# A two-layer decoder trunk: every product of the dense layers split into high and low parts, with low parts on GpSimd and vector accumulators in PSUM banks

## The reference, cut to what matters

```python
for l in range(DEPTH):                     # DEPTH = 2
    mod = silu(c) @ ada_w[l] + ada_b[l]    # shift, scale and gate of both sub-layers
    hn = rmsnorm(x) * (1 + sc1) + sh1
    xr, yr, ga, gb, gate_a, gate_b = split(hn @ w_in[l], 6)          # 1024 x 6144
    xc = short_conv(xr, 4 taps)
    h = rg_lru(xc)                         # two block-diagonal gates, then a linear recurrence
    ya = (gelu(yr) * h) @ w_branch_a[l]
    v = long_conv(ga * sigmoid(gb), 31 taps)
    yb = silu(layernorm(v)) @ w_branch_b[l] + b_branch_b[l]
    x = x + (1 + g1) * ((sigmoid(gate_a) * ya + sigmoid(gate_b) * yb) @ w_out[l])
    hn2 = rmsnorm(x) * (1 + sc2) + sh2
    x = x + (1 + g2) * (swiglu(hn2) if l == 0 else moe_top2_of_8(hn2))
y = rmsnorm(x)
```

## Time and profile before

| | us |
|---|---|
| median of 3 runs | 1646.33 (1645.79 to 1647.4) |
| the profiled execution | 1645.37 |
| its span, first to last instruction | 1643.2 |
| TensorE busy in the span | 1510.4 (92%) |
| DVE busy | 1060.5 (65%) |
| ScalarE busy | 696.6 (42%) |
| GpSimd busy | 3.6 (0%) |

### The profile page before, as it was taken

The page is one execution under the profiler, slowest core; times in us unless marked ns, Lnnn a source line. Parts: engine busy times, 40 slices in busy tenths (PEclk is TensorE's granted clock), DMA queues, the critical chain, the costliest instruction groups (busy, mean ns, idle before and its releaser), DMA issues.

```text
span 1643.2 us, 22612 instructions
## 1 busy us (share of the span) xinstructions
PE 1510.4 (92%) x8980; PEld 1291.2 (79%) x8980; DVE 1060.5 (65%) x1546; ACT 696.6 (42%) x836; POOL 3.6 (0%) x12
## 2 busy tenths in 40 slices
PE   5899999689899999989999788759999999999996
PEld 3556677579798989956777578749999999999995
DVE  2247894466544443335796477457888887898886
ACT  3134311353433332223511044335666666666662
POOL 0000000000000000000000000000000000000000
PEclk9999999789999999999999989859999999999998
DMA  9754535945476754352343944308778878877880
GB/s 343 247 179 152 207 113 109 139 129 182 194 292 230 270 179 129 116 94 86 118 125 121 86 140 146 154 36 307 285 281 305 330 277 313 324 288 284 304 319 33
DMA packets 103765, 327.32 MB, mean 199 GB/s; under 512 B 58000, under 2 KB 59408, under 8 KB 86416
## 3 DMA queue, kind: packets, MB, share of 16 engines
q1 hardware_dynamic: 103696, 326.37, 60.1%
HBM read 322.52 MB, written 3.82 MB: 199 GB/s over the span
## 4 chain that ended last, share of the span: by engine, by line
PE 84%; DVE 5%; SPq 3%; ACT 3%; DMA 3%; issue 1%; DVEq 0%; ACTq 0%
PE ps L483 23%; PE ps L466 8%; PE ps L468 7%; PE ps L467 7%; PE ps L697 6%; PE ps L698 6%; PE ps L699 6%; PE ps L663 3%; PE ps L725 3%; PE ps L727 3%; PE ps L726 3%; PE ps L508 3%; SPq L383 2%; DMA raw<-in_stream 2%; PE ps L524 2%; PE ps L516 1%
## 5 line engine op out<-in xcount | busy, mean ns | idle before, releaser
L483 PE MATMUL ps<-hn,raw 128*128 128x320 f32 x1536 | 424.5, 438 | 9.1 <-ACT hn L802 6.0
L483 PEld LDWEIGHTS ps<-hn,raw 128*128 128x128 f32 x1536 | 293.8, 192 | 137.7 <-issue 16.9
L1032 DVE TENSOR_TENSOR mlo<-mraw,mhi 128x2816 fp32r<-128x2816 f32 x108 | 332.6, 3086 | 26.1 <-ACT mhi L962 24.3
L962 ACT ACTIVATE mhi<-mraw 128x2816 fp32r<-128x2816 f32 x108 | 275.7, 2555 | 31.4 <-PE ps L699 30.1
L1032 DVE TENSOR_TENSOR wlo<-raw,whi 128x1024 fp32r<-128x1024 f32 x114 | 139.0, 1223 | 208.8 <-ACT whi L760 208.7
L1097 DVE SCALAR_TENSOR_TENSOR v<-ub,cols,v 128x320 f32<-128x320 f32 x480 | 224.4, 545 | 0.0
L760 ACT ACTIVATE whi<-raw 128x1024 fp32r<-128x1024 f32 x114 | 120.3, 1055 | 174.5 <-PE ps L468 101.4
L697 PE MATMUL ps<-mhi,xg_hi 128*128 128x352 f32 x576 | 187.6, 326 | 2.6 <-DVE xg_lo L1032 2.6
L698 PE MATMUL ps<-mlo,xg_hi 128*128 128x352 f32 x576 | 185.4, 322 | 0.0
L699 PE MATMUL ps<-mhi,xg_lo 128*128 128x352 f32 x576 | 185.3, 322 | 0.0
L466 PE MATMUL ps<-xn_hi,whi 128*128 128x320 f32 x480 | 151.6, 316 | 7.0 <-DVE xn_lo L1032 6.8
(11 more groups left out here) (218 smaller groups left out, 2138.8 us busy)
## 6 DMA issues: line engine op xcount, KB each, us to landing
mraw<-in_moe SPq DMA_DIRECT2D x108, 1408.0 KB, 6.8
raw<-in_stream SPq DMA_DIRECT2D x210, 512.0 KB, 3.6
ada<-in_ada SPq DMA_DIRECT2D x24, 2048.0 KB, 8.2
out_cc<-upad SPq DMA_DIRECT2D x18, 120.0 KB, 13.0
wrg<-in_wrg SPq DMA_DIRECT2D x2, 1024.0 KB, 19.4
upad<-in_cc SPq DMA_DIRECT2D x16, 120.0 KB, 3.3
x<-in_x SPq DMA_DIRECT2D x1, 1280.0 KB, 7.8
out_y<-bb SPq DMA_DIRECT2D x8, 160.0 KB, 1.9
```

Of the source, the lines that this page charges most:

```text
L483: mm = e.matmul(ps[s][:, 0:T], raw[:, s, k * P:(k + 1) * P], hn[:, k, :], start=k == 0, stop=k == NT - 1)
L962: e.activation(mhi[:, s % MSPL, :], mraw[:, s % MRAW, :], ACT.Copy).then_inc(m_hi, 1)
L1032: return e.tensor_tensor(out, src, hi.bitcast(F32), ALU.subtract)
```

## The change

All chunks are now split; `native` and the buffer `hn` are gone. The layer's order becomes four chunks of gates and values for the long convolution, then the short convolution's inputs, then the other gates and values. ScalarE makes every high part. The low parts of the input projection and of branch a (chunks 0 to 55 of each layer) are made by GpSimd, those of branch b, the output projection and the SwiGLU by DVE. Loads wait for these low parts.

Chunks go round three PSUM banks instead of four. The banks set free hold vector data: the running sums of both convolutions (DVE's taps now read one operand from SBUF and one from PSUM; ScalarE writes the first tap of the long one), values and merged branches that are used straight from their bank, the roots and reciprocals of the norms. ScalarE also takes over the casts to high parts of activations and one square. The first two chunks of a stage are multiplied together, tile by tile (`ramp`). The RG-LRU gates stand one pair behind each of chunks 14 to 21. The sums over v stand behind chunks 28, 38, 46 and 53, and the squares of the layer norm are summed behind chunk 55, after branch a. The state stores are issued one behind each chunk load from chunk 36 on. The adaLN slices of layer 0 use one buffer, with one slice every three chunks.

```diff
-XR, GG, YR, GA, GB, BA, BB, WO = 0, 8, 24, 32, 40, 48, 56, 64
-IN_STREAM = {XR: 16, GG: 0, YR: 24, GA: 32, GB: 48, BA: 40, BB: 56, WO: 64}
-
-NATIVE = 48
+G0, XR, G1, YR, GA, GB, BA, BB, WO = 0, 4, 12, 24, 32, 40, 48, 56, 64
+IN_STREAM = {G0: 0, XR: 16, G1: 4, YR: 24, GA: 32, GB: 48, BA: 40, BB: 56, WO: 64}
...
+BANKS = 3
...
+LO_POOL = {n: k + 1 for k, n in enumerate(n for n in range(NCHUNK) if place_of(n)[1] < BB)}
+LO_DVE = {n: k + 1 for k, n in enumerate(n for n in range(NCHUNK) if place_of(n)[1] >= BB)}
...
+        SPREADS = ({2: (0,), 3: (1,), 15: (2, 3), 23: (4, 5), 36: (6, 7)},
+                   {2: (0,), 3: (1,), 18: (2, 3), 26: (4, 5), 38: (6, 7)})
...
+        def bank(n):
+            return ps[n % BANKS][:, 0:T]
...
+            def run_and_store(l, n0, n1):
+
+                for n in range(n0, n1):
+                    chunk(L0[l] + n)
+                    if 0 <= n - 36 < 2 + NT:
+                        store_state(l, n - 36)
+                store_state(l, 2 + NT)
...
+            def low(n):
+                e.wait_ge(hi_ready, n + 1)
+                e.tensor_tensor(wlo[:, n % RING, :], raw[:, n % RING, :], whi[:, n % RING, :].bitcast(F32),
+                                ALU.subtract).then_inc(lo_pool, 1)
...
+                for n in range(RING, BB):
+                    low(L0[l] + n)
...
+            def begin(n):
+                e.wait_ge(*split_done(n))
+                if n >= BANKS:
+                    e.wait_ge(*emptied(n - BANKS))
...
+            def ramp(n, xs, ready):
+
+                begin(n)
+                begin(n + 1)
+                for k in range(NT):
+                    e.wait_ge(*ready(k))
+                    for m in (n, n + 1):
+                        mm = split_mm(bank(m), wtile(m, k), (xs[0][:, k, :], xs[1][:, k, :]), k == 0, k == NT - 1)
+                        if k == NT - 1:
+                            mm.then_inc(chunk_done, 1)
...
+                ramp(p0, xn, lambda k: (norm_ready, HN_BASE[2 * l] + k + 1))
+                slice_of(1)
+                for n in range(2, BA):
+                    paired(p0 + n, xn)
+                    slice_of(n)
+                    if 14 <= n < 22:
+                        gates(n - 14)
+                    if n in (28, 38, 46):
+                        sum_v((28, 38, 46).index(n))
...
+                    paired(p0 + n, q, (lambda k: (q_ready, 2 * l + k // 4 + 1)) if n == BA else None)
+                    if n == BB - 3:
+                        sum_v(3)
+                sum_squares()
+                ramp(p0 + BB, q, lambda k: (v_ready, NT * l + k + 1))
+                for n in range(BB + 2, WO):
+                    paired(p0 + n, q)
...
+                def evac_gate(i):
+                    if i >= 2 or l:
+                        e.wait_ge(u_ready, NT * l + i - 1)
+                    if i < 2 and l:
+                        e.wait_ge(h_ready, NF)
+                    evacuate(p0 + gate_of(i), tmp[:, i % 2, :], ACT.Sigmoid)
...
+                    e.wait_ge(spread_done, NT * l + i + 1)
+                    e.activation(segs(ps[CONV[i % 2]][:, 0:T], TS), segs(out[:], CW)[:, :, 0:TS], ACT.Identity,
+                                 scale=col("ccw", l, i), bias=col("ccb", l, i)).then_inc(seeded, 1)
...
+                    ahead(p0 + n)
+                    slice_of(n)
+                    if 14 <= n < 22:
+                        i = n - 14
+                        for w, (buf, b) in enumerate(((ab, "ba"), (bb, "bx"))):
+                            e.wait_ge(rg_done, 2 * NT * l + 2 * i + w + 1)
+                            e.activation(buf[:, i, :], ps[SHORT[w]][:, 0:T], ACT.Sigmoid, bias=col(b, l, i)
+                                         ).then_inc(rg_sig, 1)
...
+                    for i in SPREADS[l].get(n, ()):
+                        spread(i)
...
+                    if n == BB - 2:
...
+            def tap(out, src, w, acc, since=1):
+
+                if conv_n[0] > since:
+                    e.wait_ge(conv_step, conv_n[0] - since)
+                return e.scalar_tensor_tensor(out=segs(out, TS), in0=src, scalar=w, in1=segs(acc, TS), op0=ALU.mult,
+                                              op1=ALU.add)
...
+                    n = p0 + gate_of(i)
+                    e.wait_ge(evac_done, EVAC[n])
+                    e.wait_ge(chunk_done, n + 2)
+                    g, val = tmp[:, i % 2, :], bank(n + 1)
...
+                    for k in range(1, KC):
+                        for do in between.get(k, ()):
+                            do()
+                        for j in range(2):
+                            t = i + j
+                            acc = ps[CONV[j]][:, 0:T]
+                            src = segs(ub[j][:], CW)[:, :, k:k + TS]
+                            w = col("ccw", l, k * NT + t)
+                            if k == 1:
+                                e.wait_ge(seeded, NT * l + t + 1)
+                            if k < KC - 1:
+                                step(tap(acc, src, w, acc))
+                            else:
+                                tap(v[:, t, :], src, w, acc, 1 - j).then_inc(v_done, 1)
...
+                    long_conv(0, {10: (sh(0),), 14: (sh(1),), 18: (sh(2),), 22: (sh(3),), 25: (u(2),)})
+                    make_u(3)
+                    long_conv(1, {10: (u(4),), 20: (u(5),), 30: (u(6),)})
+                    long_conv(2, {2: (u(7),), 6: (decay,)})
...
+                    long_conv(0, {8: (sh(0),), 11: (sh(1),), 13: (sh(2),), 16: (sh(3),), 18: (u(2),), 25: (u(3),)})
+                    make_u(4)
+                    long_conv(1, {8: (u(5),), 15: (u(6),), 21: (u(7),)})
+                    decay()
+                    long_conv(2, {})
+                recur()
...
-                long_conv(3, {20: lambda: wlow(p0 + BA), 24: lambda: wlow(p0 + BA + 1), 28: lambda: wlow(p0 + BA + 2)})
-                for n in range(BA + 3, BA + 6):
+                long_conv(3, {})
...
+                for i in range(NT):
+                    e.scalar_tensor_tensor(out=v[:, i, :], in0=ps[5][:, 0:T], scalar=-1.0 / D, in1=v[:, i, :],
+                                           op0=ALU.mult, op1=ALU.add).then_inc(ln_cent, 1)
+                for n in range(BB, BB + 4):
                     wlow(p0 + n)
...
-                        wlow(p0 + BB + (i + 1) // 2)
...
+                    n = p0 + BB + i
+                    e.wait_ge(chunk_done, n + 1)
+                    link(e.scalar_tensor_tensor(out=bank(n), in0=bank(n), scalar=col("bbb", l, i), in1=sgb[:, i, :],
+                                                op0=ALU.add, op1=ALU.mult))
+                    e.tensor_tensor(bank(n), bank(n), gy[:, i, :], ALU.add).then_inc(m_sum, 1)
+                    e.wait_ge(m_high, NT * l + i + 1)
+                    low(1, xn_lo[:, i, :], xn_hi[:, i, :], bank(n)).then_inc(m_ready, 1)
+                    wlow(n + 4)
```

More of the change, by code:

```diff
@@ L396, in _ @@
-            store_states(0)
-            run(BA, WO)
-            e.wait_ge(out_done, STORES)
+            e.dma_start(adas[0][0][:], ada[NA]).then_inc(ada_landed[0], 16)
+            run(RING, 9)
+            for g in range(NSLICE - NA - 1):
+                e.wait_ge(ada_rows, NA + g + 1)
+                e.dma_start(adas[0][0][:], ada[NA + g + 1]).then_inc(ada_landed[0], 16)
+                run(9 + 3 * g, 12 + 3 * g)
+            run_and_store(0, 9 + 3 * (NSLICE - NA - 1), BB)
+            run(BB, WO)
@@ L560, in sum_v @@
-                def sum_v(i):
-                    e.wait_ge(conv_step, CONVS * l + C_SHORT + 2 * KC * (i // 2 + 1))
-                    return e.matmul(ps[4][:, 0:T], ones[:], v[:, i, :], start=i == 0, stop=i == NT - 1)
-                for n in range(GA):
-                    native(p0 + n, NT * 2 * l if n == 0 else None)
-                    if l == 0:
-                        if n == 1:
-                            rows(NA - 1, NA, 32, adas[0][NA - 1])
-                        if n == 2:
-                            turn(NA)
-                        if n % 4 == 3 and NA + 1 + n // 4 < NSLICE:
-                            rows(NA, NA + 1 + n // 4, 16 * (n // 4 + 1), adas[0][NA])
-                        if n % 4 == 1 and n > 4 and NA + n // 4 < NSLICE:
-                            turn(NA + n // 4)
-                    if n == 11:
-                        gates()
@@ L596, in _, with slice_of, gates @@
-                for n in range(BB, WO):
-                    paired(p0 + n, (q_hi, q_lo), (lambda k: (v_ready, NT * l + k + 1)) if n == BB else None)
+                def slice_of(n):
+                    if l == 0 and n <= 22 and n % 3 == 1:
+                        rows(0, NA + n // 3, 16 * (2 + n // 3), adas[0][0])
+                    if l == 0 and n <= 23 and n % 3 == 2:
+                        turn(NA + n // 3)
+                def gates(i):
+                    if i == 0:
+                        e.wait_ge(wrg_in, 16 * (l + 1))
+                        e.wait_ge(xc_ready, NT * (l + 1))
```

(29 more changed lines are left out.)

625 lines of the change are left out of this document (291 added, 334 removed).

## The result

The changed kernel takes 1536.45 us (median; 1534.24 to 1538.87) against 1646.06 for the kernel before: the ratio is 0.9335 with a 95% interval of 0.9318 to 0.9351. The prediction was 1542 us, faster. The profiled execution has a span of 1537.1 us, 106.1 less than before.

What follows compares the result with a forecast made beforehand. TensorE, busy 92% of the span, was taken as the bound. Gains of 59.1 us in layer 0 and 57.5 in layer 1 make 116.6; 1645.4 - 116.6 + 13 charged = 1542 us, range 1518 to 1580.

Steps and rivals of the forecast that it cites:

- rival A: Whole kernel: TensorE's chunk rate sets the pace, 1542 us, with 1522 to 1556 of its own; chance 0.62.
- charges: Taken off the gain: stores 3 + 3 us, u tiles 2, ScalarE's lumps 5; together 13 us.
- Chunk price: TensorE: a split chunk takes 3.52 us against 4.31 for a native one, 0.79 us cheaper.
- Layer 0's stretch: Layer 0's input projection on TensorE: 195.1 us against 236.0, 40.9 us less.
- The pause: TensorE idle while state stores hold SP's queue: spreading them gains 15.2 and 15.4 us, less 3 us a layer charged.
- Branch a and the layer norm: Stretch behind the input projection: 29.3 us plus a 9.2 us chain, 38.5 against 41.5, 3.0 us less a layer.
- DVE's cover: Input projections: DVE's work, with PSUM taps at 0.48 us, is just in time; 2 and some 10 us to spare.
- rival C: DVE and GpSimd sharing SBUF: each of 12 DVE instructions waits out a whole low part; 1575 us; chance 0.09.
- GpSimd's cover: GpSimd's low part takes 2.68 us, 3.7 with the high part, against 10.6 us between buffer release and use.
- Rival D: GpSimd's low part sets the pace: no gain at about 5.0 us each, 1693 us at 5.5; chance 0.07.
- Rival E: State stores stall TensorE in their new place, 15 us a layer: 24 more, 1566 us; chance 0.09.
- B: Convolution taps in PSUM come at 0.549 us on DVE: 1556 us; chance 0.13.

Runs made afterwards that it cites:

- the third edit: Changed kernel with three TensorE waits taken away; this one delays layer 1's second low part until the samples are modulated. All three together: 1532.73 us, ratio 0.9312.
- the first run: Kernel before with only the state stores moved, one behind each weight chunk from chunk 36 on, native chunks kept: 1608.16 us, ratio 0.9762.
- run 44: Not a run number: 44 counts low parts. The run meant is the changed kernel with SBUF accumulators and low parts cut to 32 columns: 1586.76 us, ratio 0.9615.

## Why the prediction came out right

The code's way was as predicted (rival A), and the time within 0.4%. Without its charges the forecast had a span of 1643.2 - 116.6 = 1526.6; the charges were 13 us, and the measured span lies 10.5 above. The parts were less right than the sum, and that it fits so closely is in part luck: the 6 us charged for the stores were not needed, and other waits, which follow, took their place.

**Chunk price: right.** 4.31 to 3.52 us. No run changes it alone: 94 chunks at 0.79 less are 74 us, and the rest of the change behind the stores is 71.7. Layer 1's stretch took 184.4 us from its first matmul against 187.3 - 1.5 = 185.8.

**Layer 0's stretch: 202.7, not 195.1.** 4.16 of the 7.6 are the last u tile. The step charged 2 us for u tiles, thinking of a DVE that is late. DVE had idled: that u stood behind pair 2's first taps, which waited 17.37 and 1.58 us for ScalarE's spreads (DVE's timeline; upad is the u tile). ScalarE made these from 175.24 on, behind sixteen tanh and exp instructions that began at 165.54: it is the lump for which 5 us were charged, and it came in by way of a u tile.

```profile
177.48 0.56 DVE L1176 SCALAR_TENSOR_TENSOR ps<-ub,cols,ps 128x320 f32<-128x320 f32 x1 [17.37 <-ACT ps L953]
179.62 0.56 DVE L1176 SCALAR_TENSOR_TENSOR ps<-ub,cols,ps 128x320 f32<-128x320 f32 x1 [1.58 <-ACT ps L953]
180.08 0.41 DVE L1238 TENSOR_TENSOR upad<-tmp,ps 128x256 f32<-128x256 f32 x1
```

Behind the wait the granted clock was lower, which cost about 2.2 more: 48 matmuls in 9.3 us by the windows, where 63 would fit at 3.52 / 24 us each.

```profile
180.70:190.00 9.30, 9.23 (x48) 9.26 (x49) 9.04 (x10) 6.45 (x8) 6.54 (x3) 0.73 0.21 58
```

**The pause: right in its cause, too small in its size.** 15.2 and 15.4 were counted; the stores alone gave 18.5 and 17.8 (292.7 to 274.2, 283.3 to 265.5). The charge of 3 us a layer for the stores in their new place was for nothing.

**Branch a and the layer norm: the step that failed.** It forecast 38.5 against 41.5, which made a gain of 3.0. But the 41.5 held the slow clock behind the pause; without the pause the old order takes 38.8. The new one takes 40.3 and 42.5. So, against the run with the stores alone, this stretch is a loss of 1.5 and 3.6. The chain is 10.9 us, not 9.2: the step counted one product of 320 columns, and DVE makes all eight (3.27 us from 300.21) ahead of the first low part. In layer 1, 1.98 more are the last pair's sum.

**Branch b and the output projection:** 0 was forecast; 61.9 to 61.0 and 60.8 to 58.0. The run with GpSimd there shows that it isn't the low parts; which of the other edits gave it was not tried.

**The starts.** Layer 0's was to stay as it was and is 2.7 us longer: the slice ahead of which TensorE waits lands later, and its matmuls start at 57.38 for 54.69. Part of it is scatter, for in the run with more low parts on GpSimd, whose code is the same up to there, they start at 55.43; the rest is open. For layer 1's, 1.5 were forecast and some 4.4 paid: the wait for the norm is 10.43 where it was 6.04. 2 of it are DVE's samples beside GpSimd's two first low parts, as the third edit shows.

**DVE's cover: right, with the margin seen.** The taps' 0.48 was 0.460, against 0.464 in SBUF, so PSUM costs a tap nothing. The Trainium skill's 125 ns of access overhead for DVE on PSUM against 60 on SBUF (Perfetto Trace Analysis, Optimizing Scalar/DVE Operations) does not show in these rows; an estimate by it was 0.529. Of waiting beside GpSimd 13 us a layer were charged; decay, recurrence and branch a took 7.7 and 36.1 us in layer 1's timeline (770.8 to 778.5 and 806.0 to 842.1), some 20 more than their lengths in the kernel before, between the charge and rival C's 32. With that DVE was just too late, once, by 1.98 us: the predicted slack of 2 in layer 1 and 10 in layer 0 had the right order.

**GpSimd's cover: right.** 2.68 us were forecast for a low part; it takes 2.41 at the median and 2.71 on the mean, and TensorE waits for one of them, once.

**Rival C** named the mechanism that the accumulators would have met, and only half of what it does. The Trainium skill (SBUF — State Buffer, Who interferes with whom) says that a DVE instruction with two SBUF inputs and a GpSimd one that reads SBUF exclude each other, and that one with a single SBUF input, outside DVE's two-port modes, does not contend. The taps agree: 0.549 us on the mean with one SBUF input, 0.819 with two beside low parts. One input is not always enough: the cast `q_hi`, which reads `gy` alone, went from 0.83 to 2.92 us; whether it ran in such a mode no run shows. **Rival D**'s break-even at 5.0 us a low part was met within 9 us by the doubled ones. **Rival E** is refuted by the first run, and B by the taps 0.460 us apart.

## What to carry to other kernels

When GpSimd takes work off DVE, look at DVE's operands first: here the whole gain of 110 us hung on the accumulators being in PSUM, so that a tap has one SBUF input; casts and small products between the taps still waited. Price a pause of TensorE with the slow chunks behind it, and before crediting a stage with a gain, ask whether its time held an after-effect of the stage ahead. When a wait for a transfer goes, follow the queue: the next transfer in it may be the next wait.

## What the runs showed of the hardware

DVE taps with two SBUF inputs, one behind the other, can keep GpSimd waiting for longer than one of them lasts. GpSimd's low parts, from the view of that tile in the two runs with SBUF accumulators, 32 columns and full width (min, median and max ns):

```profile
L515 POOL TENSOR_TENSOR wlo<-raw,whi x112: 248/273/23426, 34.2 to 911.7; 128x32 fp32r<-128x32 f32 x108, 128x1024 fp32r<-128x1024 f32 x4
```
```profile
L514 POOL TENSOR_TENSOR wlo<-raw,whi x112: 2342/2638/27355, 34.5 to 968.0; 128x1024 fp32r<-128x1024 f32 x112
```

They do not always: in the first run 44 low parts began while such a tap ran, and 27 of them took 0.70 us or less, the others 1.36 to 23.43. In the second it was mostly the tap that waited: 64 of 70 such low parts took 3.38 us or less, the others 3.68 to 27.36, and 63 of the 480 taps of the long convolution took over 2 us. The taps start every 0.464 us and last 0.54, so each begins before the one ahead has ended. That is so in both cases, and what decides between them is not shown.

In the other direction a small DVE instruction can pay nearly a whole low part: 64 columns went from 0.27 to 2.32 us, and a cast with one SBUF input from 0.83 to 2.92. After a wait of TensorE of 4.16 us the granted clock was 0.73 over 9.3 us.
